# A routed transformer trunk: the router's split weights side by side, and the expert rows fetched back two tiles sooner

## The reference

```python
def moe_swiglu(h, router_w, wg, wu, wd):
    tokens = h.reshape(b * s, d)
    probs = softmax((tokens @ router_w), axis=-1)
    top_p, top_i = lax.top_k(probs, TOP_K)
    top_p = top_p / jnp.sum(top_p, axis=-1, keepdims=True)
    ...
    for e in range(N_EXPERTS):
        y = y + gates[:, e:e + 1] * swiglu(tokens, wg[e], wu[e], wd[e])
```

## Time and profile before

| | |
|---|---|
| median of 3 runs | 2277.18 us (2272.61 to 2278.07) |
| the profiled execution | 2274.77 us |
| its span | 2273.1 us |
| TensorE busy | 2222.6 us (98%) |
| TensorE's granted clock, mean | 0.995 |
| VectorE, ScalarE, GpSimd busy | 1565.0, 1240.8, 376.3 us |
| DMA moved | 523.43 MB, of it 500.42 in SyncE's queue and 22.03 in GpSimd's |

### The profile page before, as it was taken

The page is one execution under the profiler, slowest core; times in us unless marked ns, Lnnn a source line. Parts: engine busy times, 40 slices in busy tenths (PEclk is TensorE's granted clock), DMA queues, the critical chain, the costliest instruction groups (busy, mean ns, idle before and its releaser), DMA issues. The chain is left out here.

```text
span 2273.1 us, 29218 instructions
## 1 busy us (share of the span) xinstructions
PE 2222.6 (98%) x10255; PEld 1827.2 (80%) x10255; DVE 1565.0 (69%) x1716; ACT 1240.8 (55%) x1531; POOL 376.3 (17%) x196
## 2 busy tenths in 40 slices
PE   7999999999999999999999999999999999999996
PEld 6888888888888888888877888888877888888884
DVE  4466686666655566665554456686679999999996
ACT  5445454454444444444435455454458888888885
POOL 2111221222222222222212121122210000000001
PEclk9999999999999999999999999999999999999998
DMA  7454545555555655555554454555599999999996
GB/s 245 148 194 153 185 160 188 184 171 195 180 194 185 194 193 192 195 180 189 185 185 161 154 182 148 185 186 180 186 341 362 380 384 382 380 379 379 383 384 179
DMA packets 264461, 523.43 MB, mean 230 GB/s; under 512 B 15236, under 2 KB 19464, under 8 KB 263176
## 3 DMA queue, kind: packets, MB, share of 16 engines
q1 hardware_dynamic: 259648, 500.42, 64.4%
q0 software_dynamic: 4544, 22.03, 3.0%
q10 hardware_dynamic: 200, 0.05, 0.0%
HBM read 515.10 MB, written 15.75 MB: 234 GB/s over the span
## 5 line engine op out<-in xcount | busy, mean ns | idle before, releaser
L660 ACT ACTIVATE w_hi<-raw 128x1024 fp32r<-128x1024 f32 x744 | 778.6, 1058 | 609.1 <-PE acc L1575 558.2
L999 DVE TENSOR_TENSOR w_lo<-raw,w_hi 128x1024 fp32r<-128x1024 f32 x606 | 758.0, 1270 | 477.4 <-ACT w_hi L660 475.0
L1573 PE MATMUL acc<-w_hi,a_hi 128*128 128x512 f32 x1632 | 644.4, 395 | 3.9 <-DVE w_lo L999 2.4
L1575 PE MATMUL acc<-w_hi,a_lo 128*128 128x512 f32 x1632 | 636.9, 390 | 0.0
L1574 PE MATMUL acc<-w_lo,a_hi 128*128 128x512 f32 x1632 | 636.6, 390 | 0.0
L572 POOL TENSOR_TENSOR w_lo<-raw,w_hi 128x1024 fp32r<-128x1024 f32 x138 | 337.8, 2448 | 1304.8 <-ACT w_hi L660 1005.2
L1573 PEld LDWEIGHTS acc<-w_hi,a_hi 128*128 128x128 f32 x1632 | 307.2, 188 | 67.6 <-DVE w_lo L999 3.8
L1575 PEld LDWEIGHTS acc<-w_hi,a_lo 128*128 128x128 f32 x1632 | 307.0, 188 | 65.1
L1574 PEld LDWEIGHTS acc<-w_lo,a_hi 128*128 128x128 f32 x1632 | 307.4, 188 | 61.5
L1866 PE MATMUL acc<-w_hi,a_hi 128*128 128x512 f32 x752 | 300.6, 400 | 4.2 <-DVE w_lo L999 4.1
L1868 PE MATMUL acc<-w_hi,a_lo 128*128 128x512 f32 x752 | 293.6, 390 | 0.0
(11 more groups left out here) (237 smaller groups left out, 1496.2 us busy)
## 6 DMA issues: line engine op xcount, KB each, us to landing
raw<-in_w_in SPq DMA_DIRECT2D x112, 1024.0 KB, 5.0
raw<-in_moe_w_gate SPq DMA_DIRECT2D x64, 1024.0 KB, 10.0
more_raw<-in_moe_w_up SPq DMA_DIRECT2D x64, 1024.0 KB, 10.6
raw<-in_dense_w_gate SPq DMA_DIRECT2D x44, 1024.0 KB, 5.1
raw<-in_dense_w_up SPq DMA_DIRECT2D x44, 1024.0 KB, 5.1
raw<-in_dense_w_down SPq DMA_DIRECT2D x44, 1024.0 KB, 5.2
raw<-in_w_out SPq DMA_DIRECT2D x32, 1024.0 KB, 5.3
raw<-in_moe_w_down SPq DMA_DIRECT2D x32, 1024.0 KB, 8.6
```

What stands on the lines that cost most here:

```text
L660: nc.scalar.activation(w_hi[:, slot], raw_tile(tile)[1][:, u % TILE_UNITS], ACT.Copy)\
L999: nc.vector.tensor_tensor(w_lo[:, slot], raw_tile(u // TILE_UNITS)[1][:, u % TILE_UNITS], w_hi[:, slot].bitcast(F32), ALU.subtract).then_i ...
L1573: nc.tensor.matmul(dst, hi, w_hi[:, slot, c], start=first and c == 0, stop=False)
L1575: ins = nc.tensor.matmul(dst, lo, w_hi[:, slot, c], start=False, stop=last and c == UNIT_CHUNKS - 1)
```

## The change

The thin weights' high and low parts lie side by side for each chunk, in one tensor of 16 columns. The router takes both as one stationary operand: two products per chunk (with the high and the low part of the input) in place of three, into 16 partitions, the upper eight of which hold the sums with the low weights. (The product low x low comes with it.) The logits leave PSUM with 16 partitions, and in place of the two transposes by the identity TensorE multiplies them by `fold` [16, 8], two identities of 8 on top of each other, which transposes and adds the halves in one. VectorE makes `fold` from the identity by one sum, ahead of the last quarter's low parts. The forget gates keep their three products, on views of the new tensor. And GpSimd's wait before the returning rows is for tile 20 instead of tile 22 of the last pass.

```diff
@@ -192,8 +192,9 @@
-        thin_hi = sb("thin_hi", [P, 3, CH, HEADS], F32R)
-        thin_lo = sb("thin_lo", [P, 3, CH, HEADS], F32R)
+        thin_both = sb("thin_both", [P, 3, CH, 2, HEADS], F32R)
+        thin_hi, thin_lo = (thin_both[:, :, :, n] for n in range(2))
+        fold = sb("fold", [2 * EXPERTS, EXPERTS])
...
-        rt_logits = eg[0:EXPERTS, 0, 0:BLOCKS * P]
+        rt_logits = eg[0:2 * EXPERTS, 0, 0:BLOCKS * P]
...
@@ -632,7 +634,7 @@
             pool.wait_ge(rows_out, last * 48 + 16 * NCOL)
 
-            tile_loaded(pool, M0 // TILE_UNITS + PASS_TILES - 2, PASS_UNITS, last)
+            tile_loaded(pool, M0 // TILE_UNITS + PASS_TILES - 4, PASS_UNITS, last)
             pool.sem_inc(transfer_may, 1)
@@ -761,7 +763,7 @@
                         act.wait_ge(thin_in, 16 * (DEPTH + 1))
-                        nc.scalar.activation(thin_hi[:], thin, ACT.Copy).then_inc(thin_h, 1)
+                        nc.scalar.activation(thin_hi, thin, ACT.Copy).then_inc(thin_h, 1)
@@ -885,7 +887,7 @@
-            nc.scalar.activation(rt_logits, acc[0:EXPERTS, 0, 0, 0:BLOCKS * P], ACT.Copy).then_inc(rt_copied, 1)
+            nc.scalar.activation(rt_logits, acc[0:2 * EXPERTS, 0, 0, 0:BLOCKS * P], ACT.Copy).then_inc(rt_copied, 1)
@@ -1318,6 +1320,8 @@
             nc.vector.memset(in_front[:, 0], 0.0)
+            nc.vector.tensor_tensor(fold[:], ident[0:2 * EXPERTS, 0:EXPERTS], ident[0:2 * EXPERTS, EXPERTS:2 * EXPERTS], ALU.add)\
+              .then_inc(fold_ready, 1)
             input_lo(3, 3)
@@ -1794,14 +1798,22 @@
-            logits = acc[0:EXPERTS, 0, 0, 0:BLOCKS * P]
+            logits = acc[0:2 * EXPERTS, 0, 0, 0:BLOCKS * P]
+
+            def router_products(chunks):
+
+                for k in chunks:
+                    w = thin_both[:, 2, k].rearrange("p t e -> p (t e)")
+                    nc.tensor.matmul(logits, w, a_hi[:, k], start=k == 0, stop=False)
+                    ins = nc.tensor.matmul(logits, w, a_lo[:, k], start=False, stop=k == CH - 1)
+                return ins
...
-                ins = thin_products(2, logits, range(4 * quarter, 4 * quarter + 4))
+                ins = router_products(range(4 * quarter, 4 * quarter + 4))
@@ -1812,9 +1824,10 @@
             pe.wait_ge(rt_copied, 1)
+            pe.wait_ge(fold_ready, 1)
             for b in range(BLOCKS):
-                ins = nc.tensor.transpose(acc[:, 0, 1, b * EXPERTS:(b + 1) * EXPERTS], rt_logits[:, b * P:(b + 1) * P],
-                                          ident[0:EXPERTS, 0:EXPERTS])
+                ins = nc.tensor.matmul(acc[:, 0, 1, b * EXPERTS:(b + 1) * EXPERTS], rt_logits[:, b * P:(b + 1) * P], fold[:],
+                                       start=True, stop=True)
```

More of the change, by code:

```diff
@@ L290, in trunk @@
         a_ready = sem("a_ready")
+        fold_ready = sem("fold_ready")
         f_ps = sem("f_ps")
@@ L1092, in _ @@
                         dve.wait_ge(thin_h, 1)
-                        nc.vector.tensor_tensor(thin_lo[:], thin, thin_hi[:].bitcast(F32), ALU.subtract)\
+                        nc.vector.tensor_tensor(thin_lo, thin, thin_hi.bitcast(F32), ALU.subtract)\
                           .then_inc(thin_ready, 1)
```

## The result

The median of before is 2276.50 us, of after 2280.71 us (2276.52 to 2284.21), 15 runs each; two of before's took 4565 and 5809 us and don't enter the ratio. The ratio is 1.0022, with a 95% interval from 1.0016 to 1.0029: **5.0 us slower, by 3.6 to 6.6**. The size is under the 0.3% that I had called no change, and the time lies in the range, but the interval leaves no doubt of the sign. And it isn't +1.9 by the route that I forecast. It is the sum of two effects of opposite sign, of which I had one on the wrong side and missed the other.

A forecast was written before the change was run, and what follows sets the result against it. It took TensorE, busy 98% of the span, as the bound, with the seam before the experts and the tail deciding. Router 0.0 and tail +1.9 us, placed between two bases, gave 2277.9 us, range 2272 to 2282.

The forecast's parts named there:

- The router: Before the experts: -0.46 products, +0.1 VectorE sum, +0.24 `fold` products, hidden by the wait for the first gather: 0.0 us.
- one VectorE sum of 16 x 8: Router: the added instruction making `fold`, ahead of the low parts, taken as 0.1 us later for quarter 3.
- Now they come at 2223.4: Tail: first returning rows 2.3 us after their issue, while tiles 22 and 23 still stream, 518 load packets to come.
- T: Tail: the time tile 23 lands, taken as 2251.7; the end moves by about T - 2249.8.
- One for one: Tail: load and row queues share engines packet by packet, so a row goes in front of nearly every load packet.
- 32 x 0.088 = 2.8 later: Tail: sharing with loads delays the returning rows 2.8 us, against 5.37 sooner, by themselves -2.6 us.
- no contention: Tail: sharing between returning rows and loads costs nothing, -5.4 us, 2270.6; chance 0.06.
- three signs of being wrong: Tile 23 landing by 2247, returns keeping their old pace beside the loads, or the first gather moving.
- rival 1: Tail: the last loads fit, T under 2247.2, so the rows decide: -2.6 us, 2273.4; chance 0.28.
- rival 2: Tail: no contention between rows and loads, returns keep their old pace: -5.4 us, 2270.6; chance 0.06.
- T + 10.9: Tail: TensorE's end after tile 23 lands, T + 2.4 + 6.8 + 1.7, at 2262.6.
- rival 3: Slower by more than 6.8 us; chance 0.08.

The follow-up runs named there:

- the router alone: The changed kernel with the gate of the returning rows back at tile 22, against the kernel before: ratio 1.0039, +8.9 us.
- the empty tensor: The kernel before plus an unused tensor of 32 bytes a partition where `fold` lies in the changed kernel: ratio 1.0042 against the kernel before.
- the run with tile 18: The changed kernel with `fold` behind everything and the gate at tile 18 instead of 20: 2273.11 us, ratio 0.9989 against the kernel before.

## Why the prediction was right and wrong

**The number was near by luck.** 2277.9 was forecast, 2280.71 came, inside the range. The effects behind it are -5.2 (what rows and router are worth with nothing moved) and some +10 (the moved buffers), not 0.0 and +1.9.

**The router: right.** 0.0 was the sum. The steps hold in the trace: the pitch of a product with 16 stationary columns is 0.118 us for 0.115; `fold` costs 0.14 for 0.1; its products 0.61 in four records for 0.53; the copy out of PSUM takes 0.37 us from 16 partitions, as it did from 8; the path to the slot numbers is 0.14 shorter for 0.1. The cover held (GpSimd 11.64 us, TensorE 3.4), and the router alone costs what an empty tensor costs, to within the 3 us of their intervals. The 0.46 us that quarter 0 saves did go into the wait of quarter 3's transposes: it was 0.64, and is 1.09 in the run with `fold` behind everything. (It is 0.86 in the changed kernel, where slower products stand ahead of it; the empty tensor by itself took it from 0.64 to 0.38.)

**The missing term: "one VectorE sum of 16 x 8".** I priced the instruction that makes `fold` and not the tensor. The term was in the diff, where `fold` stands ahead of `gain`: the buffers behind it, `o_hi` and `o_lo` among them, have addresses 32 bytes further in the changed kernel's program. Estimated from the pitches of one row of products, 233.3 and 226.6 ns, it is at most 1824 x 6.6 ns = 12.0 us, and it is 10.8 in the trace by the seam; the empty tensor in that place cost +9.6 us (ratio 1.0042), and taking `fold` out of it gave back 10.2 (+5.0 to -5.2, ratios 1.0022 and 0.9977). No row of the kernel before could have priced it; but the question "what moves in SBUF?" belonged among the parts of the change, with an open end of the range.

**The returning rows: the failed step is "Now they come at 2223.4".** The gate's gain was right: the first return was forecast for 2221.13, and with the shift of 11.7 that is 2232.8; it came at 2232.81. The count of loads was right too: at 2235.1, where the shift puts 2223.4, 545 load packets were left, and I had 518. But I had let the first rows come 2.3 us after their issue, which was the time behind an empty load queue. Behind loads the first came at 2236.60, after 3.8 us, and in this time the loads ran on with all 16 engines full, 624 packets in the first 3.2 us. That left 260 packets, 16 an engine and not 32. Nor did the rows step in front of each load at once. The queues from 2237 to 2238:

```profile
q1 hardware_dynamic: 114, 0.23, 59.2%
q0 software_dynamic: 12, 0.10, 47.1%
```

From 2238 to 2250 it was 75 loads beside 325 rows, and by their start times the loads now came in rounds 0.70 us apart, the time of one row: eight packets in the round at 2238.5, six at 2240.6, two at 2246.4, one each from 2247.1 to 2249.3. That fits one load for one row on each engine that still had loads (no view shows packets by engine), some 16 rounds for the last of them. I had the slowest engine let 32 rows in front of its loads and send 17 loads behind them; there were only some 16 loads left to be held up at all. Tile 23 landed at 2249.86. In the frame of the kernel before that is T = 2238.1 (2249.86 - 11.7), where I had 2251.7 and had called 2249.8 the limit.

**One for one held once the rows were there.** The sharing that I took from the stores holds in the run with tile 18: 126 rows to 125 loads from 2223 to 2228, and rather more loads than rows after that (276 to 185 up to 2236, 225 to 192 up to 2244). It didn't hold as the first rows came in: 12 to 114, above. The traces show the delay and not its reason: from the first return's issue to its first row it is 2.4 to 2.6 us in six of the seven kernels with the gate at tile 22, 3.4 in the seventh (32 bytes between `o_hi` and `o_lo`), and 3.5 to 5.4 in the seven with an earlier gate, behind loads.

**"32 x 0.088 = 2.8 later" was wrong too.** Rows did share with loads, and lost nothing over the whole; the engines that had trailed before (0.49, 0.16, 0.08) now ended with the others, which would account for it. What was left is the rival *no contention*, -5.4, to which I had given 0.06; measured in the trace -5.7. Its reason as I wrote it isn't what happened: shares of 104.9% and 69.1 + 43.0% show engines that are full. The rows kept their pace (26.7 us for the four, 27.0 before) at the cost of tile 23, which had 12 us to give. Two of my three signs of being wrong came: tile 23 before 2247 (rival 1's sign, though not its -2.6), and the returns at their old pace (rival 2's). In device time the rows' gain is less sure than in the trace: -3.6 (-5.7 to -1.6) alone, and -5.2 (-7.3 to -3.0) together with the router where nothing is moved.

**TensorE didn't stand, and its clock stayed up.** No run with the gate at tile 20 shows the 1.7 us in T + 10.9 for work lost at a lower clock. I had estimated it from the seam, where the granted clock had a mean of 0.83 over 10 us; in the changed kernel TensorE was busy for 33.6 of the 34 us from 2230 to 2264, at 1.00. Nor did rival 3 come (more than 6.8 us slower), to which I had given 0.08. A starved tail with a lower clock came at tile 18: in the profiled execution a stall of 6.1 us and a mean clock of 0.60 in the 4.6 us behind it; the medians are 3.9 us apart, with half the executions showing no loss against tile 20.

## What to carry to other kernels

In this kernel an on-chip tensor of 32 bytes a partition moved the 23 buffers declared behind it, and an empty one in that place cost 9.6 us. Laid behind everything, or padded to 256 bytes, it cost nothing that the runs tell (0.9977 in both; padded to 64 and 128 it was 1.0028 and 1.0027). So when a change adds a tensor, try it behind the hot buffers or padded, and compare the mean time of untouched products before and after (396 and 401 ns here). When untouched instructions of one operand get longer by a few nanoseconds each, look at addresses before you look at the algorithm. The transfer that was issued behind queued loads started late here, its first row 3.8 us after the issue and not 2.4, so the earlier issue cost the loads less than my count of what was outstanding had said: tile 23 landed 2.1 us before ScalarE wanted it. With the gate two tiles earlier the cushion was spent, and TensorE stood for 6.1 us in the profiled execution. Find such a tile by trying one on either side, and look at all the times and not only at their median.

## What the hardware showed that I had not expected

In these runs the time from one large fp32r product to the next (128 x 128 stationary, 512 moving) follows the distance in SBUF between the buffers of weights that are streamed and the buffers of inputs that are loaded as stationary. For the products on `o_hi` and `o_lo` the mean of all is 227.2 ns in the kernel before and 233.2 in the changed one (226.6 and 233.3 in one row of 96). In the program of the kernel before the addresses are 49280 for `w_hi`, 65664 for `w_lo`, 98432 for `a_hi`, 114816 for `a_lo`, 194176 for `o_hi` and 210560 for `o_lo`, and the distances from the first two to the other four are multiples of 256. With `o_hi` and `o_lo` moved off them by 32 bytes (the empty tensor) the mean was 233.2, by 64 it was 233.3, by 128 it was 232.5 and by 256 it was 227.2; with all inputs moved by 64, or the inputs and the weights by amounts that differ by 64, the products on `a_hi` and `a_lo` took 233.2 to 233.4 too, and with everything moved by 64 all were as before (227.0 to 228.2). In device time it is less, 9.6 us over 1824 products (5.3 ns) and 41 over 8976 (4.6 ns); in the latter run TensorE's waits shrank as the products grew, ahead of the first product of each three in the expert passes from 4.2 to 1.4 us over the whole run. A period of 128 or less is ruled out by the run with 128 (232.5 ns); distances that are multiples of 256 but not of 512 were tried once, for `o_hi` and `o_lo`, and were as good (227.2 ns).

So the two operands' places matter to each other here, by up to 2.9% of a product (233.3 ns for 226.6).

What stays open is why. The run with `o_lo` alone moved tells the load beside a product from its own operand (239 and 229 ns, above), but its third product, slower with nothing moved at it (232.3 ns for 227.3), is not explained by a rule of distance. `raw`, which the DMA engines fill and from which ScalarE and VectorE read, moved only together with everything else. So in each run that lost time its distance to the inputs had changed as well, and no run tells the two apart. The trace of the changed kernel speaks against `raw`: around 298 of the pitches of the products on `o_hi` and `o_lo` (from 0.4 us ahead to 0.1 us behind) none of ScalarE, VectorE and GpSimd touches `raw`, and their mean is 233.1 ns, for 233.3 in the others; around 506 no DMA packet of 512 bytes or more is in flight, with 233.3 for 233.2. A run with `raw` moved by itself would be the test, and there is none.
